# S5 scan stage of a two-layer hybrid decoder: GLU products ahead of the outputs, low part inside the scan, table loads reordered

## The reference, cut to what matters

```python
bu = jnp.einsum('blgk,gpk->blgp', ug, B_bar)
_, states = lax.associative_scan(combine, (a, bu), axis=1)   # x_t = A_bar x_{t-1} + bu_t
y = jnp.einsum('gkp,blgp->blgk', C_mat, states).real.reshape(Bsz, L, Dm)
y = jax.nn.gelu(y + d_skip.astype(f32) * uf).astype(u.dtype)
y1, y2 = jnp.split(y @ w_glu, 2, axis=-1)
return y1 * jax.nn.sigmoid(y2)
```

## Time and profile before

| what | value |
|---|---|
| median of 3 runs | 2138.91 us (2138.76 to 2140.07) |
| profiled execution | 2136.69 us |
| its span, first to last instruction | 2134.4 us |
| TensorE matmul busy | 2080.9 us, 97% |
| VectorE busy | 1160.6 us, 54% |
| ScalarE busy | 605.3 us, 28% |
| mean granted TensorE clock | 0.990 |

### The profile page before, as it was taken

The page is one execution under the profiler, slowest core; times in us unless marked ns, Lnnn a source line. Parts: engine busy times, 40 slices in busy tenths (PEclk is TensorE's granted clock), DMA queues, the critical chain, the costliest instruction groups (busy, mean ns, idle before and its releaser), DMA issues.

```text
span 2134.4 us, 26594 instructions
## 1 busy us (share of the span) xinstructions
PE 2080.9 (97%) x10614; PEld 1763.3 (83%) x10614; DVE 1160.6 (54%) x1669; ACT 605.3 (28%) x709; POOL 56.1 (3%) x60
## 2 busy tenths in 40 slices
PE   4999999999999999999999999999999999999998
PEld 3788888999898889888888977778878798888886
DVE  7677545645545436886445665643458554333322
ACT  2222222323323224222222333332331233222222
POOL 2000000000000000000000000000003000000000
PEclk9999999999999999999999999999998999999999
DMA  8556565523223243666554254444677223323231
GB/s 314 159 177 206 167 200 175 170 73 123 82 81 104 69 146 130 199 228 232 172 172 157 82 157 136 145 131 162 218 243 276 83 72 113 102 81 101 94 106 55
DMA packets 245377, 314.46 MB, mean 147 GB/s; under 512 B 31777, under 2 KB 218401, under 8 KB 242993
## 3 DMA queue, kind: packets, MB, share of 16 engines
q1 hardware_dynamic: 204672, 282.67, 40.2%
q10 hardware_dynamic: 40624, 30.68, 4.6%
HBM read 289.99 MB, written 27.53 MB: 149 GB/s over the span
## 4 chain that ended last, share of the span: by engine, by line
PE 74%; issue 18%; DVE 5%; DMA 1%; ACT 1%; POOL 0%; SPq 0%; ACTq 0%; POOLq 0%; DVEq 0%
PE ps L1712 18%; PE ps L1714 18%; PE ps L1713 18%; PE ps L1739 6%; PE ps L1740 6%; PE ps L1743 6%; PE ps L1992 1%; DVE ada_first L925 1%; DVE tur L1285 1%; DMA y_dram<-s_buf 1%; DVE rot L1285 0%; DMA csil<-in_c 0%; PE ps L1994 0%; DVE w_lo L915 0%; PE ps L2108 0%
## 5 line engine op out<-in xcount | busy, mean ns | idle before, releaser
L522 ACT ACTIVATE w_hi<-w_raw 128x1024 fp32r<-128x1024 f32 x352 | 345.9, 1029 | 343.9 <-PE ps L1714 247.9
L915 DVE TENSOR_TENSOR w_lo<-w_raw,w_hi 128x1024 fp32r<-128x1024 f32 x174 | 212.7, 1222 | 391.3 <-ACT w_hi L522 389.8
L1712 PE MATMUL ps<-g_hi,w_lo 128*128 128x512 f32 (+1 forms) x952 | 346.1, 364 | 0.0
L1714 PE MATMUL ps<-g_hi,w_hi 128*128 128x512 f32 (+1 forms) x952 | 345.3, 363 | 0.0
L1713 PE MATMUL ps<-g_lo,w_hi 128*128 128x512 f32 (+1 forms) x952 | 345.3, 363 | 0.0
L1712 PE MATMUL ps<-h_hi,w_lo 128*128 128x512 f32 x880 | 344.7, 392 | 0.0
L1714 PE MATMUL ps<-h_hi,w_hi 128*128 128x512 f32 x880 | 343.0, 390 | 0.0
L1713 PE MATMUL ps<-h_lo,w_hi 128*128 128x512 f32 x880 | 343.0, 390 | 0.0
L1739 PE MATMUL ps<-h_hi,w_lo 128*128 128x512 f32 x688 | 269.3, 391 | 2.0 <-DVE w_lo L915 2.0
L1740 PE MATMUL ps<-h_hi,w_hi 128*128 128x512 f32 x688 | 268.4, 390 | 0.0
L1743 PE MATMUL ps<-h_lo,w_hi 128*128 128x512 f32 x688 | 212.2, 390 | 0.0
(11 more groups left out here) (261 smaller groups left out, 2457.6 us busy)
## 6 DMA issues: line engine op xcount, KB each, us to landing
w_raw<-in_ffn_w_in SPq DMA_DIRECT2D x86, 1024.0 KB, 7.0
ada_raw<-in_ada_w SPq DMA_DIRECT2D x128, 512.0 KB, 4.6
w_raw<-in_ffn_w_out SPq DMA_DIRECT2D x32, 1024.0 KB, 5.5
w_raw<-in_ret_w_in SPq DMA_DIRECT2D x24, 1024.0 KB, 5.2
w_raw<-in_ffn_w_out SPq DMA_DIRECT2D x16, 768.0 KB, 4.4
tb<-s_rec SPq DMA_DIRECT2D x6, 2048.0 KB, 9.1
w_raw<-in_ret_w_out SPq DMA_DIRECT2D x8, 1024.0 KB, 5.4
w_raw<-in_s_w_glu SPq DMA_DIRECT2D x8, 1024.0 KB, 5.8
```

The lines of the kernel that those rows point to most:

```text
L522: copy = lambda o, i: nc.scalar.activation(o, i, ACT.Copy)
L915: V.tensor_tensor(w_lo[k % 2][:, 0:HALF, :], w_raw[k % 2][:, 0:HALF, :], raw_f32(w_hi[k % 2][:, 0:HALF, :]), ALU.subtract).then_inc(w_lo_h ...
L1712: nc.tensor.matmul(o, wl, xh, start=start, stop=False)
L1714: return nc.tensor.matmul(o, wh, xh, start=False, stop=stop)
```

## The change

On VectorE the low part of block b-2 moves into scan b, right behind the scan instruction and ahead of the turning back. On TensorE first_glu(b-2) moves ahead of outputs(b). On SyncE the second GLU pair moves behind table 7, and table 5 waits until the first load back from `y_dram` has landed.

```diff
@@ -404,13 +404,15 @@
                 table(2)
-                glu_pair(1)
                 sp.wait_ge(tile_in[KT - 1], 32)
-                for b in range(3, 6):
-                    table(b)
+                table(3)
+                table(4)
+                sp.wait_ge(yt_in[0], 16)
+                table(5)
                 for b in range(6, KT):
                     sp.wait_ge(y_done, b - 3)
                     table(b)
+                glu_pair(1)
                 glu_pair(2)
                 glu_pair(3)
@@ -1628,6 +1630,8 @@
                     st(V.tensor_tensor_scan(scanned[:], decays[:], rot[:], 0.0, M, A_))
+                    if b >= 2:
+                        output_lo(b - 2)
                     w()
                     tt(tur[0:NS], scanned[NS:P], sn[NS:P], M)
@@ -1656,8 +1660,6 @@
                 for b in range(KT):
                     scan(b)
-                    if b >= 2:
-                        output_lo(b - 2)
                 output_lo(KT - 2)
                 output_lo(KT - 1)
@@ -2166,11 +2168,11 @@
                         keep_busy((12, 6)[b])
-                    outputs(b)
                     if b == 2:
                         pe.wait_ge(w_lo_done, C_GLU + 3)
                     if b >= 2:
                         first_glu(b - 2)
+                    outputs(b)
                 first_glu(KT - 2)
```

## The result

| | before | changed |
|---|---|---|
| median | 2138.76 us (5 runs, 2135.53 to 2140.07) | 2153.57 us (5 runs, 2147.35 to 2154.96) |
| ratio to before | | 1.0068, 95% interval 1.0057 to 1.0079 |
| profiled execution | 2136.69 us | 2154.96 us |
| its span | 2134.4 us | 2152.7 us |

The change makes the kernel 14.8 us slower by the medians, 0.68% by the ratio. The profiled executions lie 18.3 us apart, because the profile of the changed kernel is of its slowest execution. Times are microseconds again, those of the form 16xx.xx counted from the span's start; S(b), E(b), y_out(b) and y_in(b) are as in the prediction. The stage begins 0.3 later in the changed kernel's span, which is neglected.

A forecast was written before the change was run, and what follows sets the result against it. TensorE is busy nearly throughout, but in the S5 scan VectorE's scans and the y_dram round trip lead. E(7) 9.2 later plus tail 1.0 gives 10.2; 2136.69 becomes 2146.9, plus 2.2 for the median 2149.1; range 2140 to 2156.

The forecast's parts named there:

- S(b): End of scan b on VectorE; S(2) forecast at 1625.85, S(3) at 1635.9.
- E(b): End of outputs(b) on TensorE; E(7) forecast at 1687.1 against 1677.9 now, 9.2 later.
- y_out(b): Store of block b's gelu to y_dram; y_out(0) forecast to take 4 instead of 9.3.
- y_in(b): Load of block b's gelu back from y_dram; 2.9 alone, 4.9 taken for y_in(3).
- tail: first_glu(7) following gelu(7) by the round trip; half clock on its matmuls costs 0 to 2.2, 1 taken.
- gain in block 0: Spread loads let y_out(0) take 4, so VectorE's idle of 3.71 before the first low part is gone.
- ring of 9.17: Low part inside the scan closes a ring through TensorE, ScalarE and VectorE: 9.17 a block, against 8.87 now.
- Block 1: ... y_in(1) at 1631.6: Table 5 and y_out(1) both land at about 1628.7, y_in(1) at 1631.6, so S(3) is 1635.9.
- the dips: Half clock on TensorE behind gaps of 3.8 and 2.4, over products and outputs(5) and outputs(7); 3 taken for each.
- y_in(2) loses its lead: Rival: table 7 issued 0.2 behind y_in(2), which lands at 1648.6; 12.4 + 1 later, 2152.3; chance 0.20.
- Ring only: Rival: the loads keep out of each other's way, leaving 9.17 a block; say 2139, no change; chance 0.20.
- block 3: y_out(3) takes 9.1, y_in(3) 4.9 with both chunks in the queue, landing at 1654.6; S(5) 1658.8 against 1654.07.

The follow-up runs named there:

- x4: Changed kernel with each table 5 to 7 released by the landing of y_in(b-4), the second GLU pair by that of y_in(4): 2141.36 us, ratio to before 1.0017.
- u1: Changed kernel with one more SyncE wait, table 6 held until y_in(1) has landed: 2146.29 us, ratio to before 1.0036.
- x3: Changed kernel with two more SyncE waits, table 6 until y_in(1) has landed, second GLU pair until y_in(3) has: 2142.88 us, ratio to before 1.0025.
- z1: Changed kernel with one more SyncE wait, the second GLU pair held until y_in(3) has landed: 2144.01 us, ratio to before 1.0042.
- y4: Kernel before with the loads of x4 and useless matmuls filling TensorE's gaps ahead of outputs(2) and outputs(7): 2134.65 us, ratio to before 0.9988.
- y3: x4 with 10 useless matmuls ahead of first_glu(5) and of first_glu(6) on TensorE: 2139.89 us, ratio to before 1.0009.
- z3: x4 with the low part put back behind the scan on VectorE, products still ahead of outputs on TensorE: 2146.50 us, ratio to before 1.0039.

## Why the prediction was right or wrong

The direction, the mechanism and the range held: 2149 was forecast, 2153.57 came, within 2140 to 2156. Step by step, against the profiled execution, the slowest of the five:

| step | forecast | after |
|---|---|---|
| tables 3 and 4 issued | 1602.7 | 1603.88 |
| y_out(0) | 4 | 4.0 |
| S(2) | 1625.85 | 1626.11 |
| y_in(1) | 2.9 | 8.9 |
| S(3) | 1635.9 | 1642.88 |
| S(4) - S(3) | 10.15 | 11.30 |
| S(5) - S(4) | 12.75 | 16.19 |
| S(6) - S(5) | 12.2 | 11.23 |
| gelu(7) - S(6) | 16.1 | 14.53 |
| tail | 1 | 0 |

The faster u_dram stores (6.4 instead of 9.0) and the gain in block 0 came as worked out, the earlier tables 1.2 later than that. The ring of 9.17 is right, shown bare by x4. The step that was mis-sized is "Block 1: ... y_in(1) at 1631.6". By the prediction's own times y_in(1) would be issued at 1628.7 and table 6 at 1625.85 + 3.94 = 1629.8, a lead of 1.1; I asked of y_in(2) but not of this one what a shorter lead would do. y_out(1) landed 1.0 later, beside table 5, the lead was 0.33, and y_in(1) took 8.9 instead of 2.9. From S(2) to S(3) the blocks lose 6.7 more than forecast.

That is not the only miss. From S(3) to S(5) another 4.6 is lost: 2.1 by the half clock on outputs(3) behind the idle of 7.8 (gelu(3) starts 6.07 behind S(3) instead of 3.94), 1.0 on y_out(3) and 1.5 on y_in(3). From S(5) on 3.5 comes back, since the dips and the tail were priced too high. These errors cancel in part, and it is partly luck that the sum, 8.1 by which the profiled shift of 18.3 exceeds the forecast of 10.2, stays as small. The changed kernel's lowest execution is 2147.35, below the predicted 2149; that the lead was enough there is not shown, as no profile of it is kept.

One reading in the prediction is wrong. It says that the by-line row names VectorE's scan lines and the round trip ahead of any matmul line. That row has three matmul lines of the products first (13.2, 12.8 and 12.7%), because its stretch runs to 1730, behind the stage. The chain over 1595 to 1692 has `tur`, the store to `y_dram` and `rot` ahead of every matmul line, and the other scan lines and the load back behind the matmuls of outputs:

```profile
by line: DVE tur L1285 11.5%; DMA y_dram<-s_buf 11.5%; DVE rot L1285 10.9%; PE ps L2108 8.4%; PE ps L2110 8.3%; issue 8.2%; DVE scanned L1630 7.9%; DMA sq<-y_dram 5.8%; PE ps L2095 5.6%; PE ps L1712 3.8%; DVE s_prev L1285 3.6%; PE ps L1713 
```

The conclusion drawn from it, that VectorE and the round trip lead in the stage, is borne out by this row.

The rival "y_in(2) loses its lead" had the right mechanism on the wrong block; y_in(2) itself was issued in a gap and took 2.9. Ring only did not occur in the changed kernel; its place is x4, which is 0.17% slower than before. In block 3 the sum took 4.9 for y_in(3) and 9.1 for y_out(3); they took 6.4 and 10.1. The rule of the Trainium skill that was weighed there (DMA: Bandwidth & Descriptors, section "Queues, rings and completion order": a DMA engine alternates between rings by packets of some 9 to 17 descriptors, so the load should pass the chunks with a handful of turns) is not borne out by the size: 6.4 and in u1 6.5 beside chunks, against 2.8 in x3 without them. The measurement decides.

The dips of the clock came where forecast, behind idles of 7.2 and 2.44, and once more behind the 7.8 that wasn't forecast. Their price was too high: 3 was taken for each, and gelu(5) follows S(5) by 6.00 and gelu(7) follows S(7) = 1690.77 by 5.36 instead of 3.94, so 2.1 and 1.4. In the tail it is nothing: first_glu(7) starts at 1703.05, 6.92 behind gelu(7), before 6.91, with matmuls 0.4 long again.

## What to carry to other kernels

When a wait moves ahead in an engine's order, list what the awaited result itself waits for; if the chain returns to the moved instruction one block earlier, it is a ring, and its length, not the engine's busy time, is the new pace. A small transfer between large ones is priced by its lead over the next large one: with a lead of 0.33 it took 8.9 here, with 0.70 it took 2.9, and nothing between was measured. A wait on the issuing queue that holds the large one until the small one has landed cost less than the meeting (u1 and x3 against the changed kernel). Moving a load "where it has time" needs the same look at what is small and urgent beside it.

## What the runs showed of the hardware that was not expected

A load of 256 KB issued 0.33 ahead of a 2 MB load landed with it, and one issued 0.70 ahead landed as if alone (one execution each). The kernels in which a race of this kind is open (the changed kernel, z1) spread over 7.6 and 11.1 from one execution to the next, u1 and x3, where it is shut, over 5.0 and 2.8. That fits a race but doesn't show one: the kernel before, whose y_in(2) has a lead of 1.05, spreads over 5.7 to 9.4 in its four groups of 9 to 26 executions.

The clock also fell without a long gap. In y4 TensorE's matmuls run on from 1616 with no idle above 0.58, and yet the granted clock is at 0.50 from 1636 to 1640, after a stretch of states and outputs alone (64 columns each); windows of y4:

```profile
1632.00:1634.00 2.00, 1.43 (x13) 1.29 (x13) 1.79 (x4) 0.00 (x0) 0.24 (x1) 1.00 0.86 358
1634.00:1636.00 2.00, 2.00 (x16) 2.00 (x16) 1.97 (x2) 0.00 (x0) 2.00 (x2) 0.76 0.28 109
1636.00:1638.00 2.00, 2.00 (x12) 2.00 (x11) 1.79 (x4) 0.00 (x0) 1.55 (x2) 0.50 0.57 129
```

So a gap is not needed. Behind the gaps of 2.0 and more that are shown here the half clock came each time, and filling the gaps of the last round kept it away in y3 and y4; behind shorter ones it came (1.69 in x3, ahead of the products of block 1) or didn't (1.74 in z3, ahead of those of block 3). What else lowers it was not tried and stays open: in the kernel before, rounds 4 to 6 have the same mix at full clock.
